# The first norm without its wait for constants, and rows of mLSTM maxima spread by DMA, in a hybrid decoder step on one Trainium2 core

## The chip, the core and the metric

The kernel runs on one core of a Trainium2 chip. The core has five engines with queues of their own: TensorE (PE in the profile, PEld its weight loads), VectorE (DVE), ScalarE (ACT), GpSimd (POOL) and SyncE (SP), which here issues nearly all DMAs. Engines wait for each other through semaphores. The metric is the time on the device of one execution in microseconds; a kernel's number is the median of its runs.

## What is computed

Two layers of a decoder for 16 learned meta tokens and 512 prompt tokens, and beside them 8 sequences of 4 new tokens: 560 columns in all, each of 1024 features. A layer is norm, input projection, two mixers side by side, output projection, norm, and a gated feed-forward part with its norms. The change touches the very first norm and the mLSTM mixer of layer 0:

```python
def rmsnorm(x, g):
    y = xf * lax.rsqrt(jnp.mean(xf * xf, axis=-1, keepdims=True) + EPS) * g

def mlstm_chunk(carry, seqs):
    b = jnp.cumsum(logf, axis=-1)
    logD = jnp.where(causal, b[..., :, None] - b[..., None, :] + logi[..., None, :], -jnp.inf)
    m_inter = b + m[..., None]
    m_t = jnp.maximum(m_inter, jnp.max(logD, axis=-1))
    w_intra = jnp.einsum('bhtd,bhsd->bhts', q, k) * jnp.exp(logD - m_t[..., None])
    num = jnp.einsum('bhts,bhsv->bhtv', w_intra, v) + ...
```

The kernel computes the mLSTM for all positions at once, in tiles of up to 128 sources by up to 272 targets. The exponent of source s and target t is a number that belongs to s plus the negative running maximum that belongs to t, cut at zero.

## The kernel before

The residual `h` lies in SBUF with features on the 128 partitions: 8 chunks of 128 x 560. The program is a row of blocks (`nc.Block()`); in each, every engine has its own list, and a block ends when all engines, SP too, have finished theirs. Semaphores order the work inside a block.

**First block** (`transposes` with `load_inputs`, L633 to L658): SP issues the identity, tokens, parameters, the first two units of input weights (`prefetch`), and last the eight constants; then it waits for these eight (L658), which ends its list. TensorE turns the tokens into `h` meanwhile.

**First norm** (`norm` with `o=None`, called at L865, its only call). It makes the sum over features of the squares of `h`, and the products `h` times gain, cut into a high and a low part (`dst[0]`, `dst[1]`, here `xn`) for projections in pieces. The reciprocal root is applied later, by the projection.
- ACT: first two casts of weight pieces (`upcoming[0]`, which is `split_high`, L242, with a wait for the weights); then for each chunk k the high part, and for k of 5 and more also the square.
- POOL: the squares of chunks 3 and 4, then `zero_gate_weights` (three memsets).
- DVE: first the two low pieces of the weights (`upcoming[1]`, `split_low`, L252); then for each k the square if k is below 3, and the low part.
- PE: for each square, in the order 3, 0, 4, 1, 5, 2, 6, 7, two column halves of 280, summed over partitions by a matrix of ones (f32, which the profile counts as two instructions each).
- SP: `load_gate_weights` waits for POOL's memsets, issues seven loads, and waits for them.

**The blocks between.** The input projection (`project`, twice), in which TensorE has matmuls queued all the time, computes the gates too. `negM`, one row of 560 negative maxima for each of the four heads, lies on partitions 0 to 3. A block of transposes follows, in which SP loads the mLSTM states (`load_mlstm_state`), and a small block that prepares them (L1201).

**The mLSTM attention** (`decayed_attention` with `mlstm=True`, L1062, called at L1230). The list `ALL` holds 32 tiles, 8 for each head. For tile i, PE makes the scores of tile i + 1 ahead, then the column sums (L1109) and the values (L1111) with the weights of tile i; DVE makes the weights (L1193) as scores times exponentials, some of them with a mask (L1186). The last tile of a head is followed by 16 narrow products with the states (L1123).

The exponents of a head are made one head ahead: `rows_of_max(hd)` spreads the row of the head over 128 partitions of PSUM by two matmuls against a column of the identity (L1080); DVE adds the number of each source and cuts at zero (`exponents`, L1167); ACT takes the exponential (L1140). `rows_of_max(hd + 1)` stands in PE's list at the first tile of head hd, after the score of its second tile. DVE's `exponents(hd + 1, b)` follow its weights of tiles 1 to 6. At the start, PE spreads head 0's row, runs four warm-up products of 512 columns (`warm(3)`), then the first score. `ebuf` holds two heads, in turn. SP stores keys, loads eight pages of cached keys into `ring` (`load_k`, slots 0 to 7), and stores values and gates (`store_kv`, L935).

## Time and profile before

| | us |
|---|---|
| median of 3 runs | 1765.58 |
| lowest and highest of them | 1760.44, 1770.26 |
| the profiled execution | 1764.44 |
| its span, first to last instruction | 1762.9 |

| engine | busy us | share of the span |
|---|---|---|
| PE | 1636.8 | 93% |
| DVE | 820.8 | 47% |
| ACT | 483.5 | 27% |
| POOL | 292.8 | 17% |

TensorE's mean granted clock over the span is 0.950 of full speed; its two levels are 1.2 and 2.4 GHz, shown as 0.5 and 1. Timeline rows give the start from the first instruction of the span. They merge neighbours of one kind: "x24" is 24 instructions, and the time behind the start is their joint stretch. The part in brackets is the engine's idle time before the row and what ended it; "issue" is time for which the profile shows no wait. A matmul's end is modelled.

### The profile page before, as it was taken

What the parts mean: (1) busy time and instruction counts of PE and PEld (TensorE: products, weight loads), DVE (VectorE), ACT (ScalarE), POOL (GpSimd) and SP (SyncE); (2) the same over time, 40 slices, a digit from 0 to 9 for tenths busy, and PEclk for the clock granted to TensorE, in tenths of its full rate; (3) what the DMA queues carried; (4) which work ended last, traced back from release to release, by engine and by line L of the source; (5) the groups of instructions that cost most, each with busy time, mean ns of one, the idle gap of its engine ahead of it and who ended that gap; (6) DMA issues with size and microseconds to landing.
All of it is one profiled execution on the core that took longest, in us unless ns stands there. A gap on an engine that the chain in (4) does not pass through costs nothing. (4 is left out here: it accounts for less than half of the span.)

```text
span 1762.9 us, 30817 instructions
## 1 busy us (share of the span) xinstructions
PE 1636.8 (93%) x12277; PEld 1515.7 (86%) x12277; DVE 820.8 (47%) x1497; ACT 483.5 (27%) x747; POOL 292.8 (17%) x370
## 2 busy tenths in 40 slices
PE   6999989888989999999999899997599999999996
PEld 5999965666668999999999799973498999999996
DVE  4332453644546634444222867327657443443225
ACT  3111321444434322222111422135234222222121
POOL 1411000400000334343000200001302333332000
PEclk8999988888999999999999999988599999999998
DMA  4232150677351132333322132211220323233311
GB/s 136 76 97 65 43 149 1 204 222 238 101 177 49 49 95 76 90 91 94 99 70 89 48 116 73 84 48 54 74 72 25 95 71 95 74 101 99 89 43 51
DMA packets 225261, 159.76 MB, mean 91 GB/s; under 512 B 17882, under 2 KB 206022, under 8 KB 225177
## 3 DMA queue, kind: packets, MB, share of 16 engines
q1 hardware_dynamic: 221896, 156.78, 30.6%
q0 software_dynamic: 3280, 1.85, 0.5%
q8 instruction: 54, 0.88, 0.2%
q14 instruction: 31, 0.25, 0.0%
HBM read 148.98 MB, written 9.88 MB: 90 GB/s over the span
## 5 line engine op out<-in xcount | busy, mean ns | idle before, releaser
L2176 ACT CAST w_high<-ring 128x1024 fp32r<-128x1024 f32 (+1 forms) x148 | 165.5, 1118 | 740.1 <-PE psum L1977 716.0
L1977 PE MATMUL psum<-mixed_high,w_high 128*128 128x280 f32 x1472 | 310.3, 292 | 15.0 <-DVE mixed_low L2373 13.0
L1977 PE MATMUL psum<-mixed_high,w_low 128*128 128x280 f32 x1472 | 312.1, 293 | 0.0
L1977 PE MATMUL psum<-mixed_low,w_high 128*128 128x280 f32 x1472 | 309.5, 292 | 0.0
L2365 DVE TENSOR_TENSOR w_low<-ring,w_high 128x1024 fp32r<-128x1024 f32 (+1 forms) x148 | 237.1, 1602 | 136.1 <-ACT w_high L2176 136.1
L1977 PEld LDWEIGHTS psum<-mixed_high,w_high 128*128 128x128 f32 x1472 | 235.6, 189 | 16.0 <-DVE w_low L2365 13.7
L1977 PEld LDWEIGHTS psum<-mixed_high,w_low 128*128 128x128 f32 x1472 | 236.2, 190 | 0.0
L1977 PEld LDWEIGHTS psum<-mixed_low,w_high 128*128 128x128 f32 x1472 | 233.8, 189 | 0.0
L2581 POOL TENSOR_TENSOR silu<-silu,rstd 128x560 f32<-128x560 f32 x44 | 61.3, 1393 | 606.3 <-DVE silu L2445 606.3
L2445 DVE TENSOR_TENSOR silu<-silu,psum 128x280 f32<-128x280 f32 x88 | 35.3, 443 | 156.2 <-PE psum L1977 154.6
L343 PE MATMUL psum<-normed_high,w_high 128*128 128x280 f32 x448 | 94.3, 292 | 0.8 <-PEq L530 0.8
L343 PE MATMUL psum<-normed_high,w_low 128*128 128x280 f32 x448 | 93.8, 290 | 0.0
L343 PE MATMUL psum<-normed_low,w_high 128*128 128x280 f32 x448 | 93.5, 290 | 0.0
L1977 PE MATMUL psum<-hidden_high_b,w_high 128*128 128x280 f32 x308 | 90.0, 292 | 0.0
L1977 PE MATMUL psum<-hidden_low_b,w_high 128*128 128x280 f32 x308 | 90.0, 292 | 0.0
L1977 PE MATMUL psum<-hidden_high_a,w_high 128*128 128x280 f32 x308 | 89.8, 292 | 0.0
L1977 PE MATMUL psum<-hidden_high_b,w_low 128*128 128x280 f32 x308 | 89.6, 291 | 0.0
L1977 PE MATMUL psum<-hidden_high_a,w_low 128*128 128x280 f32 x308 | 89.6, 291 | 0.0
L1977 PE MATMUL psum<-hidden_low_a,w_high 128*128 128x280 f32 x308 | 89.5, 291 | 0.0
L1977 PE MATMUL psum<-normed_b,w_high 128*128 128x280 f32 x320 | 87.9, 291 | 0.0
L2445 DVE TENSOR_TENSOR silu<-rstd,psum 128x280 f32<-128x280 f32 x88 | 35.3, 442 | 110.5 <-PE psum L1977 110.3
L343 PEld LDWEIGHTS psum<-normed_high,w_high 128*128 128x128 f32 x448 | 71.1, 188 | 1.2 <-issue 1.2
(491 smaller groups left out, 3201.7 us busy)
## 6 DMA issues: line engine op xcount, KB each, us to landing
ring<-in_ffn_wd SPq DMA_DIRECT2D x16, 1408.0 KB, 7.0
ring<-in_ffn_wg SPq DMA_DIRECT2D x40, 512.0 KB, 4.0
ring<-in_ffn_wu SPq DMA_DIRECT2D x40, 512.0 KB, 5.2
ring<-in_w_in_even SPq DMA_DIRECT2D x14, 1024.0 KB, 5.4
ring<-in_w_in_odd SPq DMA_DIRECT2D x12, 1024.0 KB, 5.3
ring<-in_cache_fox_k SPq DMA_DIRECT2D x44, 256.0 KB, 4.4
projected<-in_cache_fox_v SPq DMA_DIRECT2D x28, 256.0 KB, 2.9
projected<-in_cache_fox_k SPq DMA_DIRECT2D x20, 256.0 KB, 3.9
```

The costliest lines, as they stand in the source:

```text
L343: last = nc.tensor.matmul(banks[2 * tl + half][:, 0:HALF], w[:, k, :], m[:, half * HALF:(half + 1) * HALF], start=(kk == 0 and w is w_high ...
L1977: done = mm(banks[2 * tl + a][:, 0:HALF], w, m[a], start=first and s == 0, stop=last and s == 2)
L2176: nc.scalar.copy(dst, src).then_inc(w_hi[p], 1)
L2365: v.tensor_tensor(dst, src, high_.bitcast(F32), ALU.subtract).then_inc(w_lo[p], 1)
L2445: last = v.tensor_tensor(silu[:, slot, c], silu[:, slot, c] if p else rstd[:, c], banks[2 * q + a][:, 0:HALF], ALU.mult)
L2581: g.tensor_tensor(silu[:, slot, :], silu[:, slot, :], rstd[:, :], ALU.mult)
```

## The change

In the norm, the two weight casts of ACT move from the head of its list to behind the high parts of chunks 4 and 5, and the two low pieces of DVE from the head of its list to behind the low parts of chunks 5 and 6. PE takes the squares in the order 0, 1, 2, 5, 3, 6, 4, 7. The wait for the eight constants moves from the first block to the end of SP's list in the norm's block.

In the mLSTM, PE no longer spreads the maxima. SP stores `negM` to a row buffer in DRAM ahead of the state loads, and after them reads it back for heads 0 and 1, each as one row copied to 128 partitions of a part of `ring` that holds nothing then. In the attention block it does the same for heads 2 and 3, after the first eight key loads, as soon as the buffer of two heads before has been used. `exponents` waits for that load and reads SBUF; a block of sources is one instruction, where two of the six blocks took two.

```diff
--- before.py
+++ after.py
@@ -536,9 +536,6 @@
                 if o is not None:
                     for k in range(4):
                         nc.scalar.activation(sq[:, k, :], o[:, k, :], ACT.Square).then_inc(n_sqa, 1)
-                if upcoming is not None:
-                    for p in range(2):
-                        upcoming[0](act, 0, 0, p)
                 if o is not None:
                     nc.scalar.activation(eps[:, 1:2], eps[:, 0:1], ACT.Sqrt)
                     for half in range(2):
@@ -551,6 +548,8 @@
                     if o is not None:
                         act.wait_ge(n_h, KC * a + k + 1)
                     nc.scalar.mul(dst[0][:, k, :], h[:, k, :], gain(*pre, k)).then_inc(n_high, 1)
+                    if k in (4, 5) and upcoming is not None:
+                        upcoming[0](act, 0, 0, k - 4)
                     if k >= 5:
                         nc.scalar.activation(sq[:, k, :], h[:, k, :], ACT.Square).then_inc(n_sqa, 1)
 
@@ -562,7 +561,7 @@
                     if dst is not None:
                         warm(4, 8)
                 if dst is not None:
-                    for i, j in enumerate((3, 0, 4, 1, 5, 2, 6, 7)):
+                    for i, j in enumerate((0, 1, 2, 5, 3, 6, 4, 7)):
                         pe.wait_ge((n_sq, n_sqp, n_sqa)[0 if j < 3 else 1 if j < 5 else 2], j + 1 - (0 if j < 3 else 3 if j < 5 else 5))
                         for half in range(2):
                             nc.tensor.matmul(banks[6 + half][:, 0:HALF], ones[:, :], sq[:, j, half * HALF:(half + 1) * HALF],
@@ -592,9 +591,6 @@
                         if k >= 2:
                             dve.wait_ge(n_sqp, 2 * a + k - 1)
                         v.tensor_tensor(sq[:, k, :], sq[:, k, :], sq[:, k + 4, :], ALU.add).then_inc(n_pair, 1)
-                if upcoming is not None:
-                    for p in range(2):
-                        upcoming[1](dve, 0, 0, p)
                 if o is not None:
                     for half in range(2):
                         dve.wait_ge(n_root, 2 * a + half + 1)
@@ -614,6 +610,9 @@
                         dve.wait_ge(n_high, KC * b + k + 1)
                         v.scalar_tensor_tensor(out=dst[1][:, k, :], in0=h[:, k, :], scalar=gain(*pre, k),
                                                in1=dst[0][:, k, :].bitcast(F32), op0=ALU.mult, op1=ALU.subtract)
+                        if k in (5, 6) and upcoming is not None:
+                            upcoming[1](dve, 0, 0, k - 5)
+
 
 
 
@@ -655,7 +654,6 @@
             for g in range(2):
                 sp.dma_start(step_ids[0:1, 32 * g:32 * g + 32].rearrange("a (p b) -> a p b", b=4),
                              io["page_table"][4 * g:4 * g + 4].rearrange("(a b) p -> a p b", a=1)).then_inc(s_const, 16)
-        sp.wait_ge(s_const, 16 * 8)
 
     def input_loaded(pe, j):
         if j == 0:
@@ -746,6 +744,7 @@
                 sp.dma_start(gbias[dst:dst + n, :], io[src].rearrange("(a b) -> a b", b=1)).then_inc(s_gw, 16)
             sp.dma_start(m0, io["state_mlstm_m"].rearrange("b h -> h b")).then_inc(s_gw, 16)
         sp.wait_ge(s_gw, 16 * 7)
+        sp.wait_ge(s_const, 16 * 8)
 
     def zero_gate_weights(pool):
         nc.gpsimd.memset(wg, 0.0)
@@ -922,11 +921,22 @@
     nrows = place(right, "nrows", [32, 2, 128], side="right")
     s_state = sem("mlstm_state")
 
+    neg_m_rows = nc.dram_tensor("neg_m_rows", (MH, T), F32, kind="Internal").ap()
+    row_max = [ring[:, 1, 1280 + T * i:1280 + T * (i + 1)] for i in range(2)]
+    s_rowst, s_rowmax = sem("row_max_stored"), [sem("row_max_spread") for _ in range(2)]
+
+    def spread_row_max(sp, hd):
+        sp.dma_start(row_max[hd % 2], neg_m_rows[hd].unsqueeze(0).to_broadcast([128, T])).then_inc(s_rowmax[hd % 2], 16)
+
     def load_mlstm_state(sp):
+        sp.dma_start(neg_m_rows, negM).then_inc(s_rowst, 16)
         for b in range(NB):
             sp.dma_start(Cst[:, b * MH:(b + 1) * MH, :],
                          io["state_mlstm_C"][b].rearrange("h k v -> k h v")).then_inc(s_state, 16)
         sp.dma_start(nrow, io["state_mlstm_n"].rearrange("b h k -> (b h) k")).then_inc(s_state, 16)
+        sp.wait_ge(s_rowst, 16)
+        for hd in range(2):
+            spread_row_max(sp, hd)
         sp.wait_ge(s_state, 16 * 9)
     transposes(jobs, load_mlstm_state)
 
@@ -942,6 +952,9 @@
         sp.dma_start(lf_new, CS[64:72, TP:T]).then_inc(s_ln, 16)
         for s in range(2):
             load_k(sp, s)
+        for hd in (2, 3):
+            sp.wait_ge(d_e, hd - 1)
+            spread_row_max(sp, hd)
         p = io["p_fox_v"][0].rearrange("t (c e) d -> t c e d", e=2)
         for b in range(4):
             for e in range(2):
@@ -1056,7 +1069,7 @@
     EOFF = [0, 528, 928, 1200, 1344, 1360]
     ALL = [(hd, r, tile) for hd in range(MH) for r in range(2) for tile in TILES[r]]
 
-    d_bc, d_e, d_x = sem("m_rows"), sem("exponents"), sem("decays")
+    d_e, d_x = sem("exponents"), sem("decays")
     d_s, d_w, d_wu, d_numc = (sem(x) for x in ("scores", "weights", "weights_used", "num_copied"))
 
     def decayed_attention(q, k, vt, state, bufs, mlstm, decay=None, decay_s=None, lam_steps=None, beside=None,
@@ -1071,15 +1084,6 @@
         with nc.Block() as block:
             @block.tensor
             def _(pe):
-                def rows_of_max(hd):
-
-                    if hd:
-                        pe.wait_ge(d_e, hd)
-                    for r, (c0, c1) in enumerate(RANGES):
-                        at = banks[0][:, 256:512] if r == 0 else banks[1][:, 0:c1 - c0]
-                        last = nc.tensor.matmul(at, head_row(4, hd), negM[:, c0:c1], start=True, stop=True)
-                    last.then_inc(d_bc, 1)
-
                 def score(i):
                     hd, r, (b, t0, w) = ALL[i]
                     if i >= 2:
@@ -1088,15 +1092,11 @@
                     nc.tensor.matmul(banks[2 + i % 2][0:n, 0:w], k[:, hd, s0:s0 + n], q[:, hd, t0:t0 + w],
                                      start=True, stop=True).then_inc(d_s, 1)
 
-                if mlstm:
-                    rows_of_max(0)
                 warm(3)
                 score(0)
                 for i, (hd, r, (b, t0, w)) in enumerate(ALL):
                     if i + 1 < n_tiles:
                         score(i + 1)
-                    if mlstm and i % 8 == 0 and hd + 1 < MH:
-                        rows_of_max(hd + 1)
                     n = BLK[b][1]
                     c0 = t0 - RANGES[r][0]
                     first = b == 0
@@ -1156,17 +1156,12 @@
                 def exponents(hd, b):
 
                     if b == 0:
-                        dve.wait_ge(d_bc, hd + 1)
+                        dve.wait_ge(s_rowmax[hd % 2], 16 * (hd // 2 + 1))
                         v.drain()
                     s0, n = BLK[b]
                     w = 528 - 128 * b if b < SB else NS
-                    for lo, hi, bank, at in ((0, 256, 0, 256), (256, T, 1, -256)):
-                        a, z = max(s0, lo), min(s0 + w, hi)
-                        if a >= z:
-                            continue
-                        last = v.tensor_scalar(ebuf[hd % 2][0:n, EOFF[b] + a - s0:EOFF[b] + z - s0],
-                                               banks[bank][0:n, a + at:z + at], TR[0:n, b, hd:hd + 1], 0.0,
-                                               ALU.add, ALU.min)
+                    last = v.tensor_scalar(ebuf[hd % 2][0:n, EOFF[b]:EOFF[b] + w], row_max[hd % 2][0:n, s0:s0 + w],
+                                           TR[0:n, b, hd:hd + 1], 0.0, ALU.add, ALU.min)
                     if b == SB:
                         last.then_inc(d_e, 1)
```

## Rows read from the trace of the kernel before

**Rows 1.** Waits over the whole span: who <- for what: us in total, times, longest us.

```profile
PE psum L485 <- DMA tokens_in<-in_x_prompt: 0.8, 1, 0.8
```

**Rows 2.** SyncE's own waits over the whole span, same columns; SPq is its queue.

```profile
SPq L530 <- PEq L530: 4.1, 1, 4.1
...
SPq L470 <- DMA cp<-in_state_mlstm_n: 3.6, 1, 3.6
...
SPq L470 <- DMA step_ids<-in_page_table: 3.4, 1, 3.4
```

**Rows 3.** Timeline, first norm: start us, us, engine line op out<-in xcount [idle before <-releaser].

```profile
17.26 1.54 SPq L656 DMA_DIRECT2D step_ids<-in_page_table  x2
...
22.70 3.24 POOL L575 TENSOR_TENSOR projected<-h 128x560 f32<-128x560 f32 x2 [21.97 <-POOLq L470]
23.73 3.29 DVE L254 TENSOR_TENSOR w_low<-ring,w_high 128x1024 fp32r<-128x1024 f32 x2 [7.40 <-ACT w_high L250]
...
23.86 2.23 PE L568 MATMUL psum<-projected,ones 128*128 128x280 f32 x4 [7.82 <-POOL projected L575]
24.55 4.02 ACT L553 ACTIVATE normed_high<-h,cols 128x560 fp32r<-128x560 f32 x6
...
26.94 0.73 DVE L613 TENSOR_TENSOR projected<-h 128x560 f32<-128x560 f32 x1
...
27.73 8.27 PE L568 MATMUL psum<-projected,ones 128*128 128x280 f32 x28 [1.63 <-DVE projected L613]
...
30.32 4.36 DVE L615 SCALAR_TENSOR_TENSOR normed_low<-h,cols,normed_high 128x560 fp32r<-128x560 f32 x6
```

**Rows 4.** Durations in ns (min/median/max) of the w_low splits of L254.

```profile
L254 DVE TENSOR_TENSOR w_low<-ring,w_high x28: 1216/1226/2143, 23.7 to 212.0; 128x1024 fp32r<-128x1024 f32 x28
```

**Rows 5.** Stages: from:to us, length, busy us (count) of PE, PEld, DVE, ACT, POOL, PEclk, DMA, GB/s.

```profile
30.00:36.10 6.10, 6.00 (x24) 4.42 (x23) 4.68 (x7) 1.56 (x3) 0.00 (x0) 0.95 0.10 5
```

**Rows 6.** Timeline, state loads and the start of the mLSTM attention.

```profile
229.98 0.83 SPq L929 DMA_DIRECT2D cp<-in_state_mlstm_n  x1
...
241.70 1.69 PE L1080 MATMUL psum<-m_rows,ident 4*128 4x256 f32 x4 [1.60 <-PEq L1201]
...
243.32 6.53 PE L460 MATMUL psum<-ones 128*128 128x512 f32 x8
243.51 2.53 DVE L1167 TENSOR_SCALAR projected<-psum,gate_columns 128x256 f32<-128x256 f32 x8 [2.11 <-PE psum L1080]
...
247.03 5.42 SPq L998 DMA_DIRECT2D ring<-in_cache_fox_k  x8
...
249.69 0.82 PE L1088 MATMUL psum<-projected 128*128 128x256 f32 x4
...
250.43 1.20 PE L1080 MATMUL psum<-m_rows,ident 4*128 4x256 f32 x4
```

**Rows 7.** Timeline, boundaries of heads in the mLSTM attention.

```profile
266.78 0.89 DVE L1167 TENSOR_SCALAR projected<-psum,gate_columns 128x256 f32<-128x256 f32 x2 [1.94 <-PE psum L1080]
...
279.65 0.68 PE L1088 MATMUL psum<-projected 128*128 128x128 f32 x2
280.26 2.23 PE L1080 MATMUL psum<-m_rows,ident 4*128 4x256 f32 x4
...
287.12 0.62 PE L1109 MATMUL psum<-projected,small 128*4 128x272 f32 x2
...
295.99 0.47 PE L1088 MATMUL psum<-projected 128*128 128x128 f32 x2
...
300.73 0.62 PE L1109 MATMUL psum<-projected,small 128*4 128x272 f32 x2
```

**Rows 8.** Stages after two boundaries of heads, columns of rows 5.

```profile
280.20:285.40 5.20, 5.20 (x11) 2.43 (x10) 1.18 (x3) 0.04 (x1) 0.00 (x0) 0.50 0.00 0
...
296.40:299.00 2.60, 2.60 (x8) 1.27 (x8) 0.29 (x1) 0.18 (x1) 0.00 (x0) 0.58 0.00 0
```

**Rows 9.** Issue to landing of the eight loads of forget rows (L1397).

```profile
DMA to landing us min/median/max: 2.6/6.1/7.8
```

## Prediction

> **What bounds the kernel now.** I read the busy shares first (the table above): TensorE works through most of the span and no other engine comes near half of it, so an edit counts only where TensorE stands still for it or executes something less. Then the waits of the whole span: no compute engine waits for a DMA after the first transposes, where TensorE lost 0.8 us [rows 1] (its weight loads have the same wait; GpSimd has one in a side job that nobody waits for). So a microsecond won early is not taken back by a transfer that comes at a fixed time. Then SyncE's own waits: it holds the end of the first block for 3.4 us, for the last constant, while every engine is finished; in the block of the first norm it has been ready 4.1 us when TensorE ends [rows 2]. The timeline of that norm shows TensorE as its end: one chunk (two column halves, two instructions each) at 23.86, a gap, then seven chunks without a pause from 27.73 to 36.0 [rows 3]. Last, the mLSTM attention: TensorE is nearly always busy, and spreading the maxima (L1080) stands in its queue ahead of the tile that could already run [rows 6, 7].
>
> **First block and first norm.** SP's last constant is issued by 17.26 + 1.54 = 18.80; it lands 3.4 us later, at 22.2; the norm starts at 22.70, 0.5 us behind [rows 2, 3]. Without the wait the block ends with the issue, and the norm starts at 18.80 + 0.5 = 19.3: 3.4 us earlier. The wait itself moves behind the gate loads in the norm's block; only the block's end is queued behind it, and the constants land by 22.2, well before the gate loads, which wait for GpSimd's memsets: nothing. GpSimd's squares and memsets and SP's seven gate loads all move with the start and keep their 4.1 us of slack [rows 2], less what the norm is shortened further.
>
> Inside the norm, before: ACT's two casts fill the first 24.55 - 22.70 = 1.85 us, DVE's two splits 3.29, so DVE's first square comes at 26.94 + 0.73 = 27.7, and TensorE, having done GpSimd's first square, stands 1.6 us; then seven chunks set the end, 36.0 - 22.70 = 13.3 us after the start [rows 3]. After: DVE squares at once, and TensorE starts at 19.3 + 0.73 = 20.0. Chunks 0 to 2 take up to 2.23 us each, as the one at 23.86 did at half clock [rows 3], so they end at 26.7 at the latest if their squares are there. Chunk 5 needs ACT: five x_high at 4.02/6 = 0.67, a cast at 0.93, one x_high, a cast, a square at about 0.67 make 6.6 us, 25.9; the last square, two pairs later, 28.6. Five more chunks at 24 instructions in 6.0 us, 1.0 us each [rows 5], end at 30.9 to 31.7. DVE has three squares and eight x_low at 0.73 (4.36/6) and two splits at 1.22 [rows 3, 4]: 10.5 us, 29.8. The casts, now fifth in ACT's queue, start at 19.3 + 3.35 = 22.65, the moment they started before, when their weights had landed: no new wait.
>
> What speaks against this: DVE's first split beside GpSimd's squares took 2.14 us where the usual one takes 1.23, and GpSimd's pair 3.24 [rows 3, 4]. That pair now meets DVE's squares, on which TensorE waits. If all 3.24 us fell on DVE, its third square would come at 19.3 + 5 x 0.73 + 3.24 = 26.2, chunk 2 would end at 28.4, the rest at 33.4. So the end lies between 30.9 and 33.4; I take 32.0, as a split pair lost 0.9 of those 3.24 us in the row. **Gain 36.0 - 32.0 = 4.0 us; ends 2.6 and 5.1.**
>
> The Trainium skill, SBUF — State Buffer, "Who interferes with whom", says that a DVE instruction with two SBUF inputs and a GpSimd instruction that reads SBUF exclude each other for the whole instruction. The slowed split fits it, but the squares and x_low also have two inputs; by that rule each GpSimd square that gets in first costs DVE its full length, and the later end, 33.4, would be the likelier one. The total would then be 1.4 us smaller, which the range holds.
>
> **Maxima by DMA: what goes.** L1080 runs four instructions for each head. Head 0: 241.70 to 243.3, after which the warm-up runs (243.32, 6.53 us) and holds the first score until 249.69 [rows 6]. Without it the warm-up starts at 241.7: the score comes 243.32 - 241.70 = 1.6 us earlier. DVE's eight exponent instructions (2.53 us) become six; they and ACT's exponentials stay under the warm-up. The product for head 1 (250.43, 1.20 us at full clock) stands ahead of a tile whose weights DVE still works on in part of that time: between 0 and 1.2, I take 0.7 us.
>
> For heads 2 and 3 the kernel holds its own comparison, because the last head has no L1080 to issue. From the second score of a head to the start of the third tile's column sums, with the product: 287.12 - 279.65 = 7.47 us; without: 300.73 - 295.99 = 4.74 [rows 7]. The difference, 2.7 us, is more than the product's own 2.23, because it runs at half clock and the clock comes back late: 0.50 through 280.20 to 285.40, but 0.58 over only 2.6 us without it [rows 8]. Two boundaries have the product, heads 1 to 2 and 2 to 3 in the order of issue. So 2 x 2.7 = 5.4. DVE's exponents are still there, unlike in the template; they run in DVE's pauses (it stood 1.94 us in the row of 266.78) and get one instruction less for two blocks. **Stage gain 1.6 + 0.7 + 5.4 = 7.7 us.** Lower end, if the clock is as late as now and only the full-clock product is saved: 1.6 + 0.7 + 2 x 1.2 = 4.7. Upper end, if the clock does not fall at all at these boundaries (half of the 2.6 to 5.2 us at low clock): about 10.
>
> **What comes in.** In the block of token-major transposes SP issues one row store and, after the state loads, two spreads; SP now ends its issues at 229.98 + 0.83 = 230.8 and waits 3.6 us for the loads [rows 2, 6], so the spreads are issued by about 232.5, behind the loads. The store was issued first and has the nine issues as cover; that wait delays only the spreads. They are wanted at 241.5: 9 us. In the attention block, head 2's spread follows the key loads, whose issue ends at 252.45 [rows 6]; its buffer is free long before. It is wanted about when DVE stood waiting now, 266.78 - 1.94 = 264.8, less 2.3: 262.5, 10 us later. Head 3's waits for head 1's exponents, some 4 us behind, and is wanted one head later. Queued behind that wait are SP's stores of the fox values and gates; they move by about 4 us, and the stage runs on beyond 300.73 [rows 7], so nobody waits. A spread's price is not in the trace; the nearest are the eight broadcast loads of the forget rows, 2.6 to 7.8 us to landing [rows 9], 6.1 in the middle. I take 6: all hidden. If it lands after 10 us, the excess is a stall, for the pair at the start and for head 2. A gain from the DMAs themselves is excluded: they only replace.
>
> **Sum.** 4.0 + 7.7 = 11.7 us. The profiled execution took 1764.4; 1764.4 - 11.7 = 1752.7. The median of the three runs, 1765.6, would give 1753.9. I say **1753 us**.
>
> **Rivals.**
> 1. *Half of it.* The clock stays low as long as now in each head, and GpSimd's squares stall DVE's for their full length: 2.6 + 4.7 = 7.3 us, 1757. For: the clock falls at every head's end in the trace, and TensorE's first chunks in the norm get gaps. Against: the last head recovered sooner without the product. Chance 0.19.
> 2. *The clock gains more.* At other times its low stretches may be missed altogether: 5.1 + 10 = 15 us, 1749. 0.07.
> 3. *Slower: the spreads land late.* By the code a spread writes 128 rows of 2240 bytes, 2.2 times what a load of [rows 9] writes (32 rows of 4096). If landing grows with size from the longest, 7.8 x 2.2 = 17 us: DVE stalls 17 - 9 = 8 us at the start and 17 - 10 = 7 for head 2, together more than the 11.7 us won. It decides from about 15 us for a spread; at 20 the loss is 11 + 10 - 11.7 = 9 us: 1774. Against: eight state loads, not smaller, are all landed 3.6 us after SP's last issue [rows 2]. Chance 0.04.
> 4. *It doesn't do what it says.* Something else holds the first block until 22 us: 7.7 us or so remain, 1757. 0.03.
>
> **How the numbers follow.** My case has 0.67 of its own, 1750 to 1756.5 from the ends of its terms together. Half a percent is 8.8 us, about what a measurement of this kernel can tell from no change. Faster by more: my case and rival 2, 0.74; within: rivals 1 and 4, 0.22; slower: 0.04. Three runs of before spread over 10 us, so a median of a few may stand 3 us off; that widens 1749 to 1757 to 1746 to 1760.
>
> **What would show it.** Right: the first norm's first instruction near 19.3; its TensorE end near 32; SP's constant wait of 3.4 us gone; no L1080; the first score of the attention about 1.6 us sooner after the block's start; DVE not waiting on row_max; each head boundary as short as the last one's. Wrong: DVE standing on the spread, a norm whose end is DVE's or SP's, a half-clock stretch as long as before at each head, or a later stage that grows by as much.

## The result and the profile after

The changed kernel takes 1751.7 us (median of 20 executions) beside 1763.8 us for the kernel before: a ratio of 0.9937, with an interval of 0.9923 to 0.9951, so 8.6 to 13.6 us, at the medians 12.1. One of the twenty executions of the changed kernel took 4006 us; it counts in the median and not in the ratio. The profiled execution took 1748.4 us, near the shortest of the twenty; that of before took 1764.4 us. So the two traces differ by 16.1 us, and some 4 to 5 us of that are not the change. Where they come from is one of the questions below.

TensorE's share on the page (columns: busy us, share of the span, instructions) shows that it is still the bound:

```profile
PE 1626.4 (93%) x12261; PEld 1510.0 (86%) x12261; DVE 818.1 (47%) x1489; ACT 483.9 (28%) x747; POOL 293.6 (17%) x370
```

SyncE's own waits, with the columns of [rows 2]: the wait for the constants (3.4 us) is gone, the wait for the state loads has stayed (3.9 where it was 3.6), and a new one has come, for VectorE to free a spread's buffer. No compute engine waits for a spread.

```profile
SPq L530 <- PEq L530: 4.1, 1, 4.1
SPq L470 <- DMA cp<-in_state_mlstm_n: 3.9, 1, 3.9
SPq L929 <- DVE projected L1163: 2.5, 1, 2.5
```

The timeline of the first norm, as [rows 3]:

```profile
15.63 1.54 SPq L655 DMA_DIRECT2D step_ids<-in_page_table  x2
17.96 3.37 ACT L550 ACTIVATE normed_high<-h,cols 128x560 fp32r<-128x560 f32 x5 [3.24 <-PEq L470]
17.98 0.74 DVE L609 TENSOR_TENSOR projected<-h 128x560 f32<-128x560 f32 x1 [3.02 <-PEq L470]
18.05 3.23 POOL L574 TENSOR_TENSOR projected<-h 128x560 f32<-128x560 f32 x2 [17.33 <-POOLq L470]
18.75 1.54 DVE L611 SCALAR_TENSOR_TENSOR normed_low<-h,cols,normed_high 128x560 fp32r<-128x560 f32 x1
18.78 2.24 PE L567 MATMUL psum<-projected,ones 128*128 128x280 f32 x4 [4.12 <-DVE projected L609]
20.22 1.65 DVE L609 TENSOR_TENSOR projected<-h 128x560 f32<-128x560 f32 x1
21.93 9.28 PE L567 MATMUL psum<-projected,ones 128*128 128x280 f32 x28 [0.91 <-DVE projected L609]
...
29.00 0.79 DVE L611 SCALAR_TENSOR_TENSOR normed_low<-h,cols,normed_high 128x560 fp32r<-128x560 f32 x1
...
31.84 0.52 PE L343 MATMUL psum<-normed_high,w_high 128*128 128x280 f32 x2 [0.63 <-PEq L530]
```

The norm starts at 17.96 (before 22.70), 0.8 us behind SyncE's last issue; TensorE ends at 21.93 + 9.28 = 31.21 (before 36.0), so 13.25 us after the start, where it was 13.3. VectorE is through at 29.79: TensorE still sets the end. Two things stand out. Between the first chunk and the row of seven there is still a break, 0.91 us (before 1.63), and it ends with a square of VectorE's that took 1.65 us, after a low part of 1.54, where the same instructions later take 0.73 and 0.79.

The attention, the rows that answer to [rows 6] and [rows 7]: the spreads, the warm-up, the exponents, the first score, and TensorE's sums for the third tile of each head (L1109), which repeat once a head and so measure a head's period.

```profile
225.15 0.90 SPq L929 DMA_DIRECT2D ring<-neg_m_rows  x2
235.39 5.19 PE L460 MATMUL psum<-ones 128*128 128x512 f32 x8 [1.59 <-PEq L1196]
240.42 0.82 PE L1092 MATMUL psum<-projected 128*128 128x256 f32 x4
244.34 0.62 PE L1109 MATMUL psum<-projected,small 128*4 128x272 f32 x2
246.27 3.32 SPq L929 DMA_DIRECT2D ring<-neg_m_rows  x2
255.40 0.50 DVE L1163 TENSOR_SCALAR projected<-ring,gate_columns 128x528 f32<-128x528 f32 x1
259.54 0.62 PE L1109 MATMUL psum<-projected,small 128*4 128x272 f32 x2
273.14 0.62 PE L1109 MATMUL psum<-projected,small 128*4 128x272 f32 x2
286.74 0.62 PE L1109 MATMUL psum<-projected,small 128*4 128x272 f32 x2
```

From the block's first TensorE instruction to head 0's third tile it takes 244.34 - 235.39 = 8.95 us; before, that tile came at 254.37, 12.67 us after 241.70. The head periods are 15.20, 13.60 and 13.60; before 16.42, 16.33 and 13.61. So the start gives 3.7 us, the first boundary 1.2 and the second 2.7: 7.6 us, and the next stage begins 7.7 us earlier against the attention's start (60.5 us behind it, before 68.2). VectorE's exponents of 255.40 show no wait. The landing of the four spreads:

```profile
DMA to landing us min/median/max: 3.9/5.1/5.6
```

### The profile page after: what moved, and what is told of

The parts are those of the page before. It is cut to its first block and busy times, and to the rows that moved or that the text cites. A ratio compares the mean times of both kernels' runs of the same rounds, so it can differ in the third digit from the quotient of the medians.

```text
span 1746.9 us, 30782 instructions
## 1 busy us (share of the span) xinstructions
PE 1626.4 (93%) x12261; PEld 1510.0 (86%) x12261; DVE 818.1 (47%) x1489; ACT 483.9 (28%) x747; POOL 293.6 (17%) x370
## 5 line engine op out<-in xcount | busy, mean ns | idle before, releaser
L1972 PEld LDWEIGHTS psum<-mixed_high,w_high 128*128 128x128 f32 x1472 | 235.7, 189 | 16.1 <-DVE w_low L2360 13.7
```

The lines of the kernel that those rows point to most:

```text
L1972: done = mm(banks[2 * tl + a][:, 0:HALF], w, m[a], start=first and s == 0, stop=last and s == 2)
```

## The experiments

The theory: two independent gains, both in TensorE's standing still or running at the low clock; the norm's comes from its earlier start and from casts and splits moved off the front of ACT's and VectorE's queues; the attention's is TensorE's alone, more than the products' own time because narrow products keep the clock down. The rivals are at each experiment.

**The wait alone.** The kernel before with SyncE's wait moved:

```diff
-        sp.wait_ge(s_const, 16 * 8)     # end of the first block
...
+        sp.wait_ge(s_const, 16 * 8)     # behind the gate loads in the norm's block
```

> The kernel before with only the wait for the constants moved behind the gate loads; casts, splits and squares keep their old order. Theory (the norm's gain is its earlier start, and the new order gives nothing by itself, since from the norm's start to TensorE's end the trace shows 13.3 us before and 13.2 after): the norm starts at 18 to 19.3 instead of 22.7, TensorE ends 13.3 us later at 31.3 to 32.6, and the kernel gains 3.4 to 4.7 us, all that both edits of the norm give. Rival (the old order would have lost part of it, because ACT's casts would stand first and their weights have not landed at 18): the first cast waits for the ring, and TensorE ends 14.5 us or more after the norm's start.

1762.1 us, ratio 0.9979 (0.9955 to 1.0004); the kernel before took 1765.5 us beside this run and the next three. The norm starts at 18.23. The rival said that the casts, now early, would wait for their weights. They start with the norm; the row of the casts, from its timeline, has no DMA as its releaser:

```profile
18.23 1.99 ACT L250 CAST w_high<-ring 128x1024 fp32r<-128x1024 f32 x2 [2.79 <-PEq L470]
...
23.30 9.29 PE L568 MATMUL psum<-projected,ones 128*128 128x280 f32 x28 [1.63 <-DVE projected L613]
```

TensorE's row of seven chunks begins 5.07 us after the start, as before (27.73 - 22.70 = 5.03), but lasts 9.29 us where it lasted 8.27: the end is 14.4 us after the start. The start is won, and part of it is given to the clock, which stood at 0.50 to 28.2, that is 4.9 us into that row; in the profile of before it stood at 0.50 for 2.9 us of it.

**The order alone.** The kernel before with the moved casts and splits and TensorE's new list; the wait stays:

```diff
-                    for i, j in enumerate((3, 0, 4, 1, 5, 2, 6, 7)):
+                    for i, j in enumerate((0, 1, 2, 5, 3, 6, 4, 7)):
...
-                if upcoming is not None:
-                    for p in range(2):
-                        upcoming[0](act, 0, 0, p)
...
+                    if k in (4, 5) and upcoming is not None:
+                        upcoming[0](act, 0, 0, k - 4)
```

> The kernel before with only the new order in the norm (casts and splits behind chunks, squares in the new order); the first block still waits for the constants. Theory: the norm starts at 22.7 as before and TensorE ends 13.2 to 13.4 us later, near 36; the time is that of before within 0.2%. Rival (the order is worth what the prediction put on it): TensorE ends 12.7 us after the start, 0.6 us earlier than before.

1761.0 us, 0.9980 (0.9955 to 1.0004). The start is at 21.42, when the constants have landed; the row of seven chunks begins 3.97 us after it and lasts 9.65: end 13.6 us after the start. That is neither the theory's 13.2 to 13.4 nor the rival's 12.7; with the clock's share taken out (in the part on why the prediction was right) the order is worth 0.5 us, close to the rival's 0.6.

**The whole norm part.** Both edits on the kernel before.

> The kernel before with both edits of the first norm and without the maxima by DMA. Theory (the gains of norm and attention add up, as nothing later waits for a transfer): 4 to 5 us less than before, about 1759, ratio 0.997 to 0.9975; the attention's head boundaries stay as before, 7.4 us from the second score to the third tile's sums for the two that have the product. Rival (the two parts help each other, or one alone carries the result): a ratio of 1.0 or of 0.994.

1760.0 us, 0.9982 (0.9957 to 1.0006). Start 18.38, row 3.96 us after it, end 13.4 us after it. The attention is as before: the first two head periods are 17.60 and 15.09, together 32.69, where before has 32.75. The ratio's interval holds the theory's 0.997 to 0.9975 and the rival's 1.0 alike, and leaves out its 0.994.

**The rows of maxima alone.** The changed kernel with the norm and the wait as they were.

```diff
-                    for i, j in enumerate((0, 1, 2, 5, 3, 6, 4, 7)):
+                    for i, j in enumerate((3, 0, 4, 1, 5, 2, 6, 7)):
...
+        sp.wait_ge(s_const, 16 * 8)     # end of the first block again
```

> The kernel before with only the maxima by DMA; the first block waits for the constants and the norm has its old order. Theory: 7.7 us less than before, about 1756, ratio 0.9955; the stage from the first instruction of TensorE in the attention to its last shrinks by 7 to 9 us, with 2 to 3 at the start and about 2.2 to 2.7 at each of two head boundaries. Rival (part of the 16 us between the two traces is the norm's): a ratio of 0.998 or more.

1760.3 us, 0.9972 (0.9949 to 0.9996). Its timeline of TensorE:

```profile
241.73 5.15 PE L460 MATMUL psum<-ones 128*128 128x512 f32 x8 [1.60 <-PEq L1197]
...
250.63 0.62 PE L1110 MATMUL psum<-projected,small 128*4 128x272 f32 x2
...
265.83 0.62 PE L1110 MATMUL psum<-projected,small 128*4 128x272 f32 x2
...
279.43 0.62 PE L1110 MATMUL psum<-projected,small 128*4 128x272 f32 x2
```

The block starts where it did before (241.7), and everything after is the attention's own: 8.90 us to the third tile, periods of 15.20, 13.60 and 13.61, the next stage 7.7 us earlier. The medians of this part and of the norm part are 5.2 and 5.5 us under the kernel before, together 10.7 where the change has 12.1. With intervals of a quarter of a percent each, that says only that nothing speaks against their adding up; this run's interval holds the theory's 0.9955 and the rival's 0.998, and the sizes are read in the traces.

**The products put back.** The changed kernel, with the spreads by DMA, and the four narrow products of each head where they stood; nobody reads their result:

```diff
+                def ballast(hd):
+                    for r, (c0, c1) in enumerate(RANGES):
+                        at = banks[0][:, 256:512] if r == 0 else banks[1][:, 0:c1 - c0]
+                        nc.tensor.matmul(at, head_row(4, hd), negM[:, c0:c1], start=True, stop=True)
...
+                if mlstm:
+                    ballast(0)
                 warm(3)
...
+                    if mlstm and i % 8 == 0 and hd + 1 < MH:
+                        ballast(hd + 1)
```

> The changed kernel with the four products per head put back where they stood in TensorE's list, into banks that nobody reads; the maxima still come by DMA, so VectorE does not wait for them. Theory (the stage's gain is TensorE's own time, with the clock that the narrow products keep low): from a head's second score to the third tile's sums 7 to 7.5 us at two boundaries instead of 4.7 to 5.3, the first score 1.6 us or more later after the start of the warm-up, the stage 7 us longer than in the changed kernel. Rival (the gain came from VectorE, which no longer waits for PSUM and has two instructions less for each head): the boundaries stay below 5.5 us, the stage grows by less than 3.

1757.3 us, one execution. The stage takes 68.2 us, 7.7 longer than in the changed kernel and as long as before: the whole gain is gone, though VectorE still reads its rows from SBUF. The head periods are 16.37, 16.36 and 13.66. So it was TensorE's queue and clock; the rival, VectorE reading PSUM, falls. The products of its first boundary (those of the second take 2.23 too):

```profile
258.97 2.23 PE L1090 MATMUL psum<-m_rows,ident 4*128 4x256 f32 x4
```

**The same products, full height.** As above, with 128 rows in the contraction instead of four, the same columns:

```diff
-                        nc.tensor.matmul(at, head_row(4, hd), negM[:, c0:c1], start=True, stop=True)
+                        nc.tensor.matmul(at, ones[:, :], mk[:, hd, c0:c1], start=True, stop=True)
```

> As the run before it, but the products that nobody reads use all 128 rows of the array (a matrix of ones against the keys) in place of four rows; same columns, same places. Theory (TensorE's low clock after a head's end lasts longer because four rows are next to no work for it): the granted clock comes back sooner, the boundaries take 5.5 to 6.5 us instead of 7 to 7.5. Rival (the clock follows TensorE's queue and not the rows in use): the same 7 to 7.5 us.

1753.9 us, one execution; the stage is 3.6 to 4.8 us longer than in the executions that have neither these products nor a late spread, and not 7.7. The products:

```profile
256.19 1.11 PE L1090 MATMUL psum<-projected,ones 128*128 128x256 f32 x4
...
270.44 2.07 PE L1090 MATMUL psum<-projected,ones 128*128 128x256 f32 x4
```

At the first boundary the clock did not fall at all: 1.11 us for the products where the narrow ones took 2.23, and a head period of 13.01, shorter than any without products. At the second it did (16.24), and at the third, which has no products, too (14.96). The first two periods add to 29.25 us, 0.45 more than without products, though the rows of these products add to 3.2; the narrow ones add 3.9. So what a product costs here is not its own duration: the first two periods have the clock at 0.50 for 13.7 us with four rows and for 6.8 with 128. This run also has other operands (ones and keys for the identity's column and the maxima), so it does not show by itself that the rows are the reason, and why the clock held at one boundary and not at the next is open.

**Late spreads.** The changed kernel with the spreads of heads 2 and 3 at the end of SyncE's list in the attention block:

```diff
-        for hd in (2, 3):
-            sp.wait_ge(d_e, hd - 1)
-            spread_row_max(sp, hd)
...
+        for hd in (2, 3):              # behind the stores of fox values, gates and m
+            sp.wait_ge(d_e, hd - 1)
+            spread_row_max(sp, hd)
```

> The changed kernel with the spreads for heads 2 and 3 issued at the end of SyncE's list in the attention block, behind the stores of values and gates: later by about 11 us, the price of the slower rival of the prediction. Theory (a spread lands 5 us after its issue, and VectorE wants head 2's at the second tile of head 1): issued near 257, landed near 262, wanted at 255.4; VectorE stands about 6 us on row_max, TensorE behind it, and the stage is 5 to 6.5 us longer; head 3's is still in time. Rival (there is slack behind VectorE, as TensorE works through the head's end): less than 2 us.

1756.9 us, one execution. The rival of the prediction made real, in its timeline:

```profile
258.66 0.83 SPq L929 DMA_DIRECT2D ring<-neg_m_rows  x2
263.04 0.49 DVE L1163 TENSOR_SCALAR projected<-ring,gate_columns 128x528 f32<-128x528 f32 x1 [6.94 <-DMA ring<-neg_m_rows]
264.03 1.07 PE L1109 MATMUL psum<-projected,small 128*4 128x272 f32 x2 [3.21 <-DVE projected L1188]
```

VectorE stands 6.94 us, TensorE 3.21, and the head period grows to 18.49. The next one is 16.49, though by then nothing waits for a DMA: the third tile's sums take 0.88 there and 0.62 in the changed kernel, so the low clock lasted longer a second time. The stage is 6.4 to 7.6 us longer than in the executions without a late spread, and 5 to 6.5 had been expected: one stall cost twice.

**TensorE's old list.** The changed kernel with one line undone, in one execution and then in a second, timed:

```diff
-                    for i, j in enumerate((0, 1, 2, 5, 3, 6, 4, 7)):
+                    for i, j in enumerate((3, 0, 4, 1, 5, 2, 6, 7)):
```

> The changed kernel with TensorE taking the squares in the old order 3, 0, 4, 1, 5, 2, 6, 7; casts and splits stay behind the chunks. Theory (what the new order of work gives is that TensorE's unbroken row of products begins 3.9 us after the norm's start instead of 5.0; that comes from VectorE's squares, which no longer stand behind the splits, not from TensorE's list): TensorE's first product waits for GpSimd's square, 1.2 us or, if VectorE gets in first, 1.9 us after the start, and its end is within 0.5 us of the changed kernel's, 13.2 to 13.7 us after the start. Rival (the order in TensorE's list carries the gain): its end is 14.1 us or more after the start, as with the old casts.

1749.7 us, one execution. The expectation was missed: the end came 12.0 us after the start (18.12 to 30.13), sooner than with the new list. TensorE starts later, at 19.92, but then runs 32 instructions in one row, 10.21 us. The same program in its second execution:

> The changed kernel with TensorE's old list of squares, the same program as in the look at the old list, in a second profiled execution and timed. The first look gave an end 12.0 us after the norm's start, where four executions with the new list gave 13.2 to 13.4; one execution can't say whether the list did that or a chance of the clock.
> Theory A (the list did it: TensorE starts 1.1 us later, at GpSimd's first square, but then has no break, and the clock comes back sooner after an unbroken start): again one unbroken row of 32, end 11.8 to 12.4 us after the start, the next block's first product near 30.8 in place of 31.84.
> Theory B (one execution's clock): an end 13.0 to 13.7 us after the start, with the clock back at about the time at which it comes back with the new list (26 to 27).
> The whole: 1748 to 1752 by either, ratio 0.992 to 0.9945.

This text compares with "13.2 to 13.4" for the new list; read over all six executions that have it with the moved casts, the end came 12.2 to 13.6 us after the start (13.25, 13.62, 13.42, 12.47, 12.24, 12.61; mean 12.9). The second execution of the old list, in its timeline:

```profile
19.50 10.40 PE L567 MATMUL psum<-projected,ones 128*128 128x280 f32 x32 [4.16 <-POOL projected L574]
```

One row again, end 12.2 us after the start (17.70), as theory A had it. But that does not settle it for the list: three of the six with the new one end at 12.2 to 12.6 too, which theory A did not allow for. The difference of the means is 0.8 us, and most of it is the clock, as the part on why the prediction was right shows: at the same clock the lists are 0.1 us apart. The time, 1756.4 us (the kernel before took 1769.8 beside it) or a ratio of 0.9933 (0.9908 to 0.9958), can't tell it from the change.

**No squares by GpSimd.** ScalarE makes the squares of chunks 3 and 4 too; TensorE's list is 0 to 7:

```diff
-                    if k >= 5:
+                    if k >= 3:
                         nc.scalar.activation(sq[:, k, :], h[:, k, :], ACT.Square).then_inc(n_sqa, 1)
...
-                    for k in (3, 4):
-                        nc.gpsimd.tensor_tensor(sq[:, k, :], h[:, k, :], h[:, k, :], ALU.mult).then_inc(n_sqp, 1)
```

> The changed kernel with one edit in the first norm: ScalarE makes the squares of blocks 3 and 4 too, GpSimd none, and TensorE's list is 0 to 7. It asks whether VectorE's slow instructions at the start of the norm in the changed kernel (the low part 1.54 us where later ones take 0.79, the second square 1.65 where the third takes 0.73), and with them TensorE's break of 0.91 us after the first square's products, come from GpSimd's two squares beside them (18.05 to 21.28).
> Theory (they do): the first low part takes 0.79 and the second square 0.73; the second square is ready at about 20.3, before TensorE has ended the first square's products (about 21.0), so TensorE runs all 32 in one row without a break. ScalarE's last square comes later (worked out from its rows: eight high parts of 0.75, two casts of 1.03 and five squares of 0.67, 11.4 us from 18.0, so 29.4), and TensorE ends after it, at 30.0 to 30.6, that is 12.0 to 12.6 us after the norm's start where the changed kernel needs 13.2.
> Rival (the first instructions of a block are slow by themselves, or it is ScalarE's reading of the same block that slows them): low part and square stay at about 1.5 and 1.6 us, the break stays at about 0.9 us, and TensorE's end stays at 13 us after the start or more.

1755.2 us, one execution. The norm in its timeline:

```profile
18.73 0.80 DVE L610 SCALAR_TENSOR_TENSOR normed_low<-h,cols,normed_high 128x560 fp32r<-128x560 f32 x1
18.75 10.75 PE L567 MATMUL psum<-projected,ones 128*128 128x280 f32 x32 [3.45 <-DVE projected L608]
19.45 0.74 DVE L608 TENSOR_TENSOR projected<-h 128x560 f32<-128x560 f32 x1
...
30.14 0.52 PE L343 MATMUL psum<-normed_high,w_high 128*128 128x280 f32 x2 [0.64 <-PEq L530]
```

The low part takes 0.80 and the second square 0.74, and TensorE's break is gone: it was GpSimd. The end is 11.6 us after the start (17.94), even sooner than expected, as ScalarE was done at 27.96 and not at 29.4. The next block begins 1.7 us before the changed kernel's; 0.6 us of that remain at the same clock. At the second projection 0.2 us of that are left; why, is told below.

**A warm-up between.** Six products of 512 columns, which nobody reads, after the first transposes; once with the new list and once with the old one:

```diff
+                if loaded is not None:
+                    pe.wait_ge(free[1], n0[1] + 4)
+                    warm(7, 6)
```

> The changed kernel with six products of 512 columns that nobody reads, after the first transposes, in the 3.3 us in which TensorE is idle and in which its granted clock falls to 0.5 (14.66 to 18.0); by the twelve of the same kind at the kernel's start (7.28 us, 0.61 each) they last 3.6 us, and so put the norm's start off by some 0.4 us. It asks how much of the norm's length in the changed kernel is the low clock.
> Theory (the norm's TensorE is slow because it starts at half clock; a square's four products take 1.12 us there, twice what they take at full clock): the granted clock stays at 1.00, the first four products take about 1.1 in place of 2.2, TensorE then waits for each square, and ends about 0.9 us after the last square (26.87), at 27.5 to 28.5, that is 9 to 10 us after the norm's start in place of 13.2. The next block's first product then is set by VectorE's last low part (29.8): 30.3 to 30.9 where the changed kernel has 31.84, a gain of 1 to 1.5 us there, some 0.1% of the whole, which the ratio can hardly show.
> Rival (the norm's length is in the order of the squares and the hand-over between engines): TensorE's end stays within 0.5 us of 13.2 us after the start, and the next block starts later than 31.84 by the 0.4 us of the warm-up.

> The kernel with the six warm-up products after the first transposes, and TensorE's list of squares as it was in the kernel before (3, 0, 4, 1, 5, 2, 6, 7); beside the run with the warm-up alone it differs by the list only. It asks what the order is worth when the clock is up.
> Theory (order matters only through when TensorE's first row begins and breaks, and with the clock up both lists end after the same last square): TensorE begins at GpSimd's first square, about 20.0, ends within 0.3 us of the run with the warm-up alone, and the next block's first product is at the same 30.3 to 30.9, set by VectorE's last low part.
> Rival (the old list is better by itself, as the 12.0 us against 13.2 us with the clock down might say): the next block starts 0.5 us or more ahead of the run with the warm-up alone. Counter-rival: the old list is worse by itself, by 0.5 us or more, as was said before the change ran.

1753.7 us (0.9915, 0.9883 to 0.9948) and 1757.5 us (0.9920, 0.9891 to 0.9950), the kernel before taking 1769.8 us beside them: not to be told from the change or from each other. The first mistake is in the edit's price: the page counts twelve instructions for six products, so they take 5.34 us and not 3.6, and the norm starts at 20.81 and 20.45. With the new list:

```profile
21.63 1.21 PE L570 MATMUL psum<-projected,ones 128*128 128x280 f32 x4 [1.10 <-DVE projected L612]
...
24.78 8.31 PE L570 MATMUL psum<-projected,ones 128*128 128x280 f32 x28 [1.94 <-DVE projected L612]
```

The first chunk runs at full clock (1.21 us, and not the 2.24 that the changed kernel's took at half clock), TensorE then waits 1.94 us for the square that GpSimd holds up, and the granted clock is at 0.57 from 24.0 to 28.0: the end is 12.3 us after the start, not 9 to 10. With the old list:

```profile
22.25 4.04 PE L570 MATMUL psum<-projected,ones 128*128 128x280 f32 x16 [2.07 <-POOL projected L577]
...
26.99 4.04 PE L570 MATMUL psum<-projected,ones 128*128 128x280 f32 x16 [0.70 <-ACT projected L557]
```

The clock stays at 1.00 in both rows, the end is 10.6 us after the start, and VectorE (11.8) now sets the block's end. The next block's first product comes at 32.92 where the new list has 33.81, and 0.4 us of that is the earlier start. By the numbers this is the rival, the old list as the better one; but the pair does not compare the lists at the same clock. With the new list the clock fell while TensorE waited and was at 0.50 for the first 2.9 us of the long row, which costs 1.5 of the 1.7 us between the two ends. Whether the longer wait made it fall, one execution of each can't show. The warm-up puts the start off by 2.4 to 2.7 us (against 18.1, the mean without it) and wins back 0.7 us of the new list's 12.9 and 1.5 of the old one's 12.1: no gain.

## Why the prediction was right

**Total.** 11.7 us were forecast, the medians give 12.1. The mechanism was right: every step of the sum is found in the traces, 3.1 + 0.5 for the norm and 3.7 + 3.9 for the attention, 11.2 us, inside the ratio's 8.6 to 13.6. That the attention's 7.7 came out so closely is luck, two errors that cancel.

**Start of the norm: 3.4 forecast, 3.1 found.** With the wait, three executions start at 22.70, 21.42 and 22.08, 3.9 to 4.0 us behind the end of SyncE's last issue; without, nine start between 17.70 and 18.38, 0.8 us behind it, where the prediction took 0.5. So the wait was worth 3.1 to 3.2 us. The means of the starts (22.1 and 18.1) lie 4.0 us apart, but the rest is older than the wait: SyncE's last issue ends at 17.4 to 18.8 in the three and at 16.9 to 17.6 in the nine, because one earlier issue, which blocked SyncE for 3.87 us in the profile of before, took 2.40 to 3.43 in the other thirteen executions (2.61 in the changed kernel's). Nothing of the edit stands ahead of that issue, so this is taken as chance.

**The order: 0.6 forecast, 0.5 found, once the clock is taken out.** TensorE's end lies 14.2 us after the start in the mean with the old norm and 12.9 with the new one, which looks like 1.2 us; in the two profiled executions none of it shows (13.3 and 13.25). Both are blurred by the granted clock. It is at 0.50 early in every norm here without the extra warm-up and comes back to 1.00 at another moment in each execution (read from each trace's granted clock):

| norm | clock back, us after the start | TensorE's end, us after the start | end less half of the time to the clock's return |
|---|---|---|---|
| old casts, old list (3) | 7.9, 10.0, 11.0 | 13.3, 14.4, 14.8 | 9.3 to 9.4 |
| moved casts, new list (6) | 6.8, 7.3, 7.6, 8.9, 9.2, 9.6 | 12.2, 12.5, 12.6, 13.3, 13.4, 13.6 | 8.8 |
| moved casts, old list (2) | 6.7, 7.1 | 12.0, 12.2 | 8.7 |
| moved casts, no squares by GpSimd (1) | 6.8 | 11.6 | 8.2 |

The norm of the kernel before, of the run with the rows of maxima alone, of the changed kernel and of the old list's second execution, columns of [rows 5] (the granted clock is the column behind POOL's):

```profile
22.70:36.00 13.30, 10.51 (x32) 7.35 (x32) 10.95 (x13) 8.87 (x13) 4.51 (x5) 0.70 0.13 5
22.08:36.91 14.83, 12.03 (x32) 8.33 (x32) 10.94 (x13) 8.88 (x13) 4.52 (x5) 0.63 0.12 4
17.96:31.21 13.25, 11.51 (x32) 7.98 (x32) 11.78 (x13) 8.91 (x13) 4.50 (x5) 0.67 0.24 33
17.70:29.90 12.20, 10.40 (x32) 7.67 (x32) 11.77 (x13) 8.91 (x13) 4.50 (x5) 0.72 0.27 40
```

Within each kind of norm, a microsecond more at 0.50 is half a microsecond more in length. What is left over is the order's own worth: moving casts and splits gives 0.7 us, the new list takes 0.1 back, 0.5 together. Whether an order also makes the clock come back sooner is not shown. The prediction's step that chunks 0 to 2 run through and chunk 5 waits for ACT was too smooth: TensorE broke off behind chunk 0, for VectorE.

**GpSimd against VectorE.** That square was 0.92 us longer than its sisters and the low part before it 0.75, together 1.67 us, where the prediction took 0.9 and feared 3.24. The run without GpSimd's squares shows that they are the cause. The Trainium skill, SBUF — State Buffer, "Who interferes with whom", says that a VectorE instruction with two inputs in SBUF contends with a GpSimd instruction that reads SBUF, and that the port they share is an exclusive lock. By that rule, as an estimate with GpSimd's 3.23 us in halves, VectorE's low part would end at 18.05 + 1.62 + 0.79 = 20.5 and its square at 21.28 + 0.73 = 22.0; the rows say 20.3 and 21.9. The trace agrees to 0.2 us. But the pair's 3.23 us hold waiting of GpSimd's own: in the kernel before, the first of its squares ran while VectorE stood idle and took 1.11 us, the second met VectorE's split and took 2.16 (ns, min/median/max):

```profile
L575 POOL TENSOR_TENSOR projected<-h x2: 1109/1636/2164, 22.7 to 23.8; 128x560 f32<-128x560 f32 x2
```

So, as an estimate from that row, the pair holds 2.2 us of work that VectorE could lose to, and the prediction's 3.24 was too much to fear; it lost 1.67.

**Start of the attention: 1.6 + 0.7 forecast, 3.7 found.** Without L1080 the warm-up does not only begin sooner, it is shorter: 5.19 us where [rows 6] have 6.53. Over all runs it takes 5.91 to 6.75 us behind narrow products, 5.15 to 5.53 without them, and 5.02 behind full-height ones. The step that moved the warm-up by 1.6 us kept its length, and so missed 1.3 us; with the product for head 1 (0.7 forecast, 0.8 found) that makes 1.4.

**Two boundaries: 2 x 2.7 forecast, 1.2 + 2.7 found.** The template, the last head, fits the second boundary (periods of 13.60 and 13.61) and not the first (15.20). There the clock falls sooner. Stages of the changed kernel, columns of rows 5, for the sixteen products of four columns at the end of heads 0 and 1:

```profile
251.40:254.20 2.80, 2.80 (x18) 2.80 (x17) 0.50 (x2) 0.00 (x0) 0.00 (x0) 0.63 0.99 224
266.60:268.40 1.80, 1.80 (x18) 1.80 (x17) 0.50 (x2) 0.00 (x0) 0.00 (x0) 1.00 0.00 0
```

At head 0's end the sixteen products already run at 0.63 and take 1.0 us longer than at head 1's. This is not chance: in the seven executions that have neither the products nor a late spread the first two periods add to 28.6 to 28.9 us, and in the five with narrow products to 32.7. The single periods shift between the two (16.4 + 16.3, or 17.6 + 15.1), the sum does not. So 3.9 us is the steady worth of both boundaries: less than the 2 x 2.23 that the products' rows show, more than the 2 x 1.2 that they take at full clock. The granted clock accounts for it. The first two periods of the kernel before, of the changed kernel and of the run with full-height products:

```profile
254.37:287.12 32.75, 32.75 (x141) 18.66 (x140) 12.60 (x45) 4.42 (x10) 0.00 (x0) 0.79 0.20 48
244.34:273.14 28.80, 28.80 (x133) 16.93 (x132) 10.67 (x40) 4.42 (x10) 0.00 (x0) 0.82 0.41 113
247.02:276.27 29.25, 29.25 (x141) 17.59 (x140) 10.66 (x40) 4.42 (x10) 0.00 (x0) 0.88 0.34 95
```

The clock was at 0.50 for 13.7 us of them in all five executions with narrow products, for 9.8 to 10.2 in the seven without, and for 6.8 with full-height ones. Less half of that, the periods come to 25.9, 23.7 and 25.8 us: two groups of products cost 2.2 us at full clock, whatever their height, and the narrow ones 1.7 more through 3.4 us more at the low clock. The stage's 7.7 us was right in sum because 1.4 us too little at the start met 1.5 us too much here.

**The spreads: hidden, as said.** 6 us to landing were taken; they took 3.9 to 5.6. Head 2's was issued at 246.27, and VectorE read it at 255.40 without a wait. The rival of late spreads needs a late place in SyncE's list, as its run showed: then it costs 6.4 to 7.6 us.

**The 4 to 5 us that are not the change.** SyncE's issues ahead of the wait are 1.6 us of the 16.1: they ended at 18.80 in the profile of before and at 17.17 in that of the changed kernel. Between the projections stands a stage of 48 products with the gate weights (two of the next stage fall into the windows below), with a gap of 3.45 us ahead of it in every execution. The changed kernel, and then the kernel before:

```profile
134.30:140.72 6.42, 6.40 (x50) 6.42 (x51) 0.00 (x0) 0.00 (x0) 1.06 (x2) 1.00 0.73 207
```

```profile
138.86:146.77 7.91, 7.91 (x50) 7.91 (x51) 0.00 (x0) 0.00 (x0) 1.90 (x2) 0.78 0.64 168
```

The same work takes 6.4 us at full clock and 7.9 when the clock falls in it. In two of the fourteen profiled executions it did not fall, and the profile of the changed kernel is one of them: 1.5 us of the 16.1. In the norm the clock came back 1.0 us later in the changed kernel's profile, which takes 0.5 back. It is also why the 1.7 and 1.3 us that the runs without GpSimd's squares and with the old list won at the norm are down to 0.2 here: one throw of the clock outweighs them. Another 2 us come behind 330 us, in parts that the change does not touch: the difference of the two traces is 14.0 us at the start of the stage behind the attention and wavers between 14.2 and 17.3 from 420 us on. Where these come from is open. The same chance shows in the times: the changed kernel took 1748.4 us in an execution with a mean granted clock of 0.955 and 1762.8 us in one with 0.945.

## What to carry to other kernels

Where TensorE is the bound and stands still for a moment, price a removed instruction by the period of the loop around it, measured with and without it, and not by its own duration: here two groups of narrow products of 2.23 us each were worth 3.9 us together, full-height ones in their place cost 0.45 (and 1.4 in the head behind them, in the one execution there is), and the group ahead of the warm-up took 1.3 us more than its own time. Price a removed wait from the event just ahead of it in the same execution (here SyncE's last issue: 3.1 us), since the starts of different executions differ by chance too (4.0 us). Before two orders of work are compared, take the time at the low clock out of both: the 0.8 us by which TensorE's old list seemed to win shrank to 0.1.

## What the hardware showed beside that

- The granted clock (0.5 is the 1.2 GHz level, 1.0 the 2.4 GHz one) was low for 13.7 us of the first two head periods with products of four rows (five executions), for 9.8 to 10.2 us with none (seven) and for 6.8 us with ones of 128 (one execution, with other operands).
- Where TensorE is busy without a break, a microsecond at the low level costs half a microsecond: the lengths of norms and of head periods of one kind, less half of it, agree within 0.1 us from execution to execution.
- A stall is paid twice: the late spread's 3.3 us in one head were followed by 2.9 us in the next, in which TensorE never stood still and the clock was low for 9.7 us in place of 3.4.
- One row of a DRAM tensor spread over 128 partitions (280 KB) landed in 3.9 to 5.6 us in the changed kernel, close to the state loads of 256 KB issued beside it (4.8 in the middle); over all ten executions that have spreads it took 3.9 to 6.0, and 7.1 for one issued late.
